# The recurrence of one mixer: the small matmuls of its two halves side by side

## The reference

```python
def step(state, inp):
    r_t, w_t, k_t, v_t, a_t, b_t = inp
    sa = jnp.einsum('bhij,bhj->bhi', state, a_t)
    state = (state * w_t[:, :, None, :] + sa[..., None] * b_t[:, :, None, :]
             + v_t[..., None] * k_t[:, :, None, :])
    return state, jnp.einsum('bhij,bhj->bhi', state, r_t)
```

## Time and profile before

| | |
|---|---|
| median of 3 runs | 2454.88 us (2453.4 to 2459.74) |
| profiled execution, its own time | 2453.9 us |
| its span in the trace | 2452.1 us |
| PE busy | 2248.4 us (92%) |
| DVE busy | 1281.4 us (52%) |
| ACT busy | 467.0 us (19%) |
| POOL busy | 848.7 us (35%) |
| chain that ended last, by engine | PE 79%, DVE 12%, DMA 4%, ACT 3%, issue 2% |

### The profile page before, as it was taken

The page is one execution under the profiler, slowest core; times in us unless marked ns, Lnnn a source line. Parts: engine busy times, 40 slices in busy tenths (PEclk is TensorE's granted clock), DMA queues, the critical chain, the costliest instruction groups (busy, mean ns, idle before and its releaser), DMA issues.

```text
span 2452.1 us, 27262 instructions
## 1 busy us (share of the span) xinstructions
PE 2248.4 (92%) x10664; PEld 1788.8 (73%) x10664; DVE 1281.4 (52%) x1822; ACT 467.0 (19%) x897; POOL 848.7 (35%) x1009
## 2 busy tenths in 40 slices
PE   8889978999979999999888999999997689999995
PEld 8667767778858888878656878787776348878784
DVE  3574646435473432574454754636563746727274
ACT  1210410110010000210363211102201652202021
POOL 1232313222324444444202444444433014444442
PEclk9998989998889999999889999999999889999998
DMA  8574848456979999988506889898877018989895
GB/s 261 101 159 107 171 90 175 93 113 162 289 192 211 191 193 196 193 176 184 113 1 134 189 178 195 180 197 177 193 156 154 1 43 189 192 184 193 176 193 127
DMA packets 121351, 393.59 MB, mean 161 GB/s; under 512 B 25172, under 2 KB 27348, under 8 KB 120712
## 3 DMA queue, kind: packets, MB, share of 16 engines
q0 software_dynamic: 96624, 350.46, 67.6%
q1 hardware_dynamic: 24600, 41.39, 5.3%
HBM read 387.92 MB, written 3.92 MB: 160 GB/s over the span
## 4 chain that ended last, share of the span: by engine, by line
PE 79%; DVE 12%; DMA 4%; ACT 3%; issue 2%; POOL 0%; SPq 0%; DVEq 0%; ACTq 0%
PE ps L1460 64%; PE ps L1501 3%; DMA w_lo<-in_w 2%; PE ps L1566 2%; PE ps L1547 2%; PE ps L1582 2%; DVE small L787 1%; DVE work L612 1%; PE ps L1714 1%; ACT arena L1400 1%; DMA w_hi<-in_w 1%; ACT arena L1408 1%; DVE arena L814 1%; PE ps L1658 1%; DVE arena L613 1%
## 5 line engine op out<-in xcount | busy, mean ns | idle before, releaser
L1460 PE MATMUL ps<-h_hi,w_hi 128*128 128x512 f32 x1760 | 706.0, 401 | 28.0 <-DVE h_lo L456 19.8
L1460 PE MATMUL ps<-h_lo,w_hi 128*128 128x512 f32 x1760 | 689.0, 391 | 0.0
L1460 PE MATMUL ps<-h_hi,w_lo 128*128 128x512 f32 x1760 | 688.6, 391 | 0.0
L372 POOL DMA_DIRECT2D w_hi<-in_w x334 | 185.8, 556 | 1436.9 <-PE ps L1460 1400.4
L1460 PEld LDWEIGHTS ps<-h_hi,w_hi 128*128 128x128 f32 x1760 | 332.6, 189 | 117.0 <-issue 26.2
L1460 PE MATMUL ps<-g_hi,w_hi 128*128 128x512 f32 (+1 forms) x880 | 347.3, 395 | 41.5 <-DVE g_lo L410 24.8
L1460 PEld LDWEIGHTS ps<-h_lo,w_hi 128*128 128x128 f32 x1760 | 333.1, 189 | 70.2 <-issue 4.4
L1460 PEld LDWEIGHTS ps<-h_hi,w_lo 128*128 128x128 f32 x1760 | 332.6, 189 | 70.7
L377 POOL TENSOR_SCALAR w_lo<-w_hi 128x1024 fp32r<-128x1024 f32 x334 | 361.0, 1081 | 29.0 <-DMA w_hi<-in_w 23.0
L1460 PE MATMUL ps<-g_lo,w_hi 128*128 128x512 f32 (+1 forms) x880 | 341.6, 388 | 0.0
L1460 PE MATMUL ps<-g_hi,w_lo 128*128 128x512 f32 (+1 forms) x880 | 341.1, 388 | 0.0
(11 more groups left out here) (372 smaller groups left out, 2057.6 us busy)
## 6 DMA issues: line engine op xcount, KB each, us to landing
w_hi<-in_w POOLq DMA_DIRECT2D x334, 512.0 KB, 4.0
w_lo<-in_w POOLq DMA_DIRECT2D x334, 512.0 KB, 5.7
arena<-in_ada SPq DMA_DIRECT2D x48, 512.0 KB, 6.2
x<-in_xT SPq DMA_DIRECT2D x1, 2048.0 KB, 12.1
x<-in_xT SPq DMA_DIRECT2D x4, 512.0 KB, 6.3
arena<-in_memT SPq DMA_DIRECT2D x2, 1024.0 KB, 5.8
out_y<-arena SPq DMA_DIRECT2D x1, 2048.0 KB, 6.3
arena<-s_kernels SPq DMA_DIRECT2D x8, 128.0 KB, 5.0
```

Source lines behind the costliest of these rows:

```text
L372: pool.dma_start(w_hi[:, q % SLOTS, :], A["w"][q]).then_inc(S(f"high_in{q % SLOTS}"), 16)
L1460: mm = pe.matmul(bank, w[:, slot, cols], a(k), start=(k == 0 and i == 0), stop=(k == blocks - 1 and i == 2))
```

## The change

In a step, the small matmuls of the two halves are written next to each other: L1759 for both halves, then L1760 for both; L1770 for both, then L1772 for both; and in the group o L1775 for both, L1776 for both and then L1774 for both. L1774 becomes the last of its sum instead of the first, so the flags `start` and `stop` move. The two waits for the new state (one ahead of each half) become one wait for both halves ahead of the first.

```diff
             for c in range(NCK):
                 now = c % 2
+                need("state_set", 2 if c else 1)
                 for p in range(2):
-                    need("state_set", 1 if c or p == 0 else 0)
                     pe.matmul(ps[4 + p][rows[p], 0:HD], bd["akT"][rows[p], c, :], bd["vt"][rows[p], c, :], start=True, stop=False)
+                for p in range(2):
                     pe.matmul(ps[4 + p][rows[p], 0:HD], pad("a")(p, c), state[:, now, p, :], start=False, stop=True).then_inc(S("rec_y"), 1)
                 next(steps, None)
@@
                 for p in range(2):
                     pe.matmul(ps[4 + p][:, at_s], bd["kt"][rows[p], c, :], bd["vt"][rows[p], c, :], start=True, stop=False)
+                for p in range(2):
                     need("rec_sa_copied1" if p else "rec_sa_copied")
                     pe.matmul(ps[4 + p][:, at_s], rw_bt[rows[p], c, :], chain_y[rows[p], 1, :], start=False, stop=True).then_inc(S("rec_state"), 1)
                 for p in range(2):
-                    pe.matmul(ps[6 + p][rows[p], at_o], pad("r")(p, c), state[:, now, p, :], start=True, stop=False)
-                    pe.matmul(ps[6 + p][rows[p], at_o], bd["rbT"][rows[p], c, :], chain_y[rows[p], 1, :], start=False, stop=False)
-                    mm = pe.matmul(ps[6 + p][rows[p], at_o], bd["rkT"][rows[p], c, :], bd["vt"][rows[p], c, :], start=False, stop=True)
+                    pe.matmul(ps[6 + p][rows[p], at_o], bd["rbT"][rows[p], c, :], chain_y[rows[p], 1, :], start=True, stop=False)
+                for p in range(2):
+                    pe.matmul(ps[6 + p][rows[p], at_o], bd["rkT"][rows[p], c, :], bd["vt"][rows[p], c, :], start=False, stop=False)
+                for p in range(2):
+                    mm = pe.matmul(ps[6 + p][rows[p], at_o], pad("r")(p, c), state[:, now, p, :], start=False, stop=True)
                 mm.then_inc(S("rec_o"), 1)
                 next(steps, None)
```

## The result

| | before | changed |
|---|---|---|
| median, 17 runs each, same chip | 2459.74 us (2453.4 to 2469.49) | 2443.15 us (2436.17 to 2453.15) |
| profiled execution, its own time | 2453.9 us | 2436.17 us |
| its span | 2452.1 us | 2434.4 us |
| PE busy | 2248.4 us | 2229.5 us |

The ratio is 0.9934, with a 95% interval of 0.9918 to 0.9949: faster by 16.2 us, and by 12.5 to 20.2 us at the ends of the interval. The forecast effect, 18.2 us, lies inside. The forecast time, 2436 with a range of 2432.5 to 2441, does not hold the median of 2443.15.

What follows compares the result with a forecast made beforehand. TensorE's instruction order was taken to bound the recurrence. 15 steps saving 17.0 us plus 1.2 in the first made 18.2: 2453.9 to 2435.7, put down as 2436 since the median ran 1.0 higher; range 2432.5 to 2441.

Steps and rivals of the forecast that it cites:

- What bounds the stage: Recurrence, 428 to 548 us: TensorE's own instruction order is the bound, PE busy for all 120.00 us at clock 1.00.
- The two prices: Small matmuls on TensorE: 0.11 us per further matmul in a half, 0.15 per shape change; a directly following second half free.
- y: First small-matmul group of a recurrence step: pairing the halves takes it from 1.03 to 0.52 us, 0.51 saved.
- The rule of the Trainium skill: Weight loads overlap running matmuls only in different row groups, so the state matmuls' second half would add 0.11 us.
- o: Last small-matmul group of a recurrence step: pairing the halves takes it from 1.26 to 0.63 us, 0.63 saved.
- state: Group between sa and o: the halves already overlap, so 0.60 us stays; zero gain, bounds -0.1 to +0.05 per step.
- The joined wait: Ahead of y, one wait for both halves' new state: 2.09 us of cover falls to 1.46, so it costs nothing.
- The first step: First of 16 recurrence steps, at the lower clock level: y saves 0.43 to 0.81 us, o 0.63; 1.2 taken.
- Sum: Whole recurrence: 15 steps save 17.0 us, the first 1.2, in all 18.2; nothing behind the stage eats it.
- the rival of the state pairs: In y and o, state matmuls of both halves do not overlap: 0.22 us less saved per step, about 2439.5; chance 0.08.
- other halves: Rival in y and o: halves never overlap to separate banks, only shape changes go; 9.4 us, about 2445; chance 0.04.
- the cover: Rival in the recurrence: cover gone, gain turns into waits on DVE or ACT; below 7.4 us, about 2450; chance 0.05.

Runs made afterwards that it cites:

- one state group: Changed kernel with the r x state matmul pair moved from the end of o to the end of y, beside a x state; ratio to before 0.9931.
- same columns: Changed kernel with half 1's state matmul of y written to partitions 0 to 63, as half 0's; output not the reference's; step 6.89 us.
- the repetitions: Both kernels run again unedited: the changed kernel, median 2445.29 us, ratio 0.9929; the kernel before, 2464.76 us in its profiled execution.
- state_only: Kernel before with only the group state reordered, L1770 of both halves ahead of both L1772; ratio 1.0003.
- y_only: Kernel before with only the group y paired and one wait for both halves; ratio to before 0.9964.

## Why the prediction was right, and where it failed

- *What bounds the stage.* Right. PE was gapless before and is after, so what it saved was gained.
- *The two prices.* Right. 0.11 us for a further matmul in the same half was measured as 0.12 (one state group) and 0.11 (same columns); a change of shape, put at 0.15, as 0.15 (one state group); the second half, put at nothing, costs 0.01.
- *y.* 0.51 forecast, 0.50 measured. The rule of the Trainium skill that spoke against it, named under the kernel with the same columns, does not hold here.
- *o.* 0.63 forecast, 0.61 to 0.62 measured.
- *state.* Put at zero, measured at 0.01 by itself.
- *The joined wait.* 1.46 us of cover forecast, 1.48 on the timeline. The copy of y (L640) is done 1.16 us ahead of sa (1.19 forecast), with one exception told below.
- *The first step.* 1.2 us forecast. It took 10.6 and 10.1 us before and 9.0 and 8.2 after, so 1.1 to 2.4, since the clock comes up at another moment each time.
- *Sum.* 18.2 us forecast. The recurrence went from 127.9 to 109.5 us (18.4) and, in the repetitions, from 127.3 to 108.5 (18.8). The profiled execution fell from 2453.9 to 2436.17, where 2435.7 was worked out. The comparison of runs gives 16.2 us (12.5 to 20.2) and 17.5 (12.0 to 23.1): within the intervals this is the same as 18.2, and neither says that something was given back.
- *The step that failed* is the last one, "the median of the runs shown is 1.0 us above that execution, so I put down 2436", with its term "some 1.5 us that runs differ". It took a median of three runs as the level of the kernel. In 17 runs that level is 2459.74, 4.9 us higher, and single runs spread over 16 us (2453.4 to 2469.49). The median came out 7.15 us above the 2436 put down: 4.86 of it is this level, 0.7 the rounding down of 2436.7, and 1.6 the difference between the 18.2 forecast and the 16.6 by which the medians lie apart, which is inside the interval of the effect. The level alone would have put the forecast at 2441.5, just past the end of the range. The three runs shown already spread over 6.3 us, four times the 1.5 allowed; and the profiled execution was at the low end of them. With 5 us in place of the 1.5 the range would have reached 2444.5, counted as it was from the 2439.5 of the rival of the state pairs, and held the median; from the forecast's own bounds it would have reached 2441.8 and still missed it. Where the level comes from is known in part only: executions differ most in the attention stages and at some waits of TensorE, as shown above.
- *The rivals.* The state pairs do overlap, other halves do too, the cover was enough, and the clock in the stage stayed at 1.00.

## What to carry to other kernels

Small fp32 matmuls that follow each other on TensorE with the same shape of rows and columns, in halves that share no rows or no columns, ran at the price of one (into different banks in the changed groups, into one bank in L1714). So order loops with the half innermost and count the changes of shape: between the small shapes each cost 0.15 us at the full clock. Then look for the same pattern elsewhere: an exchange of two loops in a stage nobody had looked at gave 10 us in its trace, against 18 for the recurrence. And take the level of a kernel from the spread of its runs, not from a median of three: here the effect in the trace of its stage was worked out to 1 us (18.2 against 18.4 and 18.8), while three runs gave the level only to 5.

## What was not expected of the hardware

One DVE instruction of the loop, L638 (128x64, from SBUF to SBUF), takes 0.25 us; in both profiles of the changed kernel one of its 32 took 1.61 us. In the timeline it coincides with POOL's split of the weights:

```profile
469.64 1.90 DVE L638 TENSOR_SCALAR work<-work,small 128x64 f32<-128x64 f32 x2
470.13 1.06 POOL L377 TENSOR_SCALAR w_lo<-w_hi 128x1024 fp32r<-128x1024 f32 x1
...
471.57 0.22 DVE L640 COPY work<-ps 64x64 f32<-64x64 f32 x1
```

The two L638 are over at 471.54, 0.35 us after POOL's instruction, and the copy of y behind them is done at 471.79, still 0.68 us ahead of sa (472.47), where the prediction had 1.19 us of slack. In the two profiles of before the longest L638 is 0.38 us. The other profiles bear the coincidence out. In the ten profiles of kernels with o paired, every L638 that overlaps such a POOL instruction (L377), one or two in each, takes 1.34 to 1.62 us; in the four others (before, its repetition, state_only, y_only) none overlaps one, and the longest is 0.38. So the shorter step moved the two engines onto each other. What the two share was not tested. The longer L638 took 0.5 us of the slack in that one step, which a further shortening should keep in view.
